# One decoder step on Trainium2: expert pairs in the order gate/up a, gate/up b, down a, down b

## What is computed

```python
logits = xf @ w_router + b_router
top_logit, top_idx = lax.top_k(logits, 4)
gates = softmax(top_logit)
# for each expert e, on the tokens that chose it:
gu = x_e @ w_gate_up[e] + b_gate_up[e]          # (tokens, 1024) @ (1024, 2048)
g, u = split(gu);  g = min(g, 7);  u = clip(u, -7, 7)
act = (u + 1) * g * sigmoid(1.702 * g)
y_e = act @ w_down[e] + b_down[e]               # (tokens, 1024) @ (1024, 1024)
y[tokens of e] += gates * y_e
x = layer_norm(alpha * x + y)
```

## Time and profile before

| | |
|---|---|
| median of 3 runs | 1364.59 us (1364.25 to 1365.44) |
| profiled execution, its time | 1363.42 us |
| its span, first to last instruction | 1361.6 us |
| mean granted TensorE clock | 0.966 of full |
| TensorE busy | 1213.2 us (89%) |
| VectorE, ScalarE busy | 370.0 us, 204.2 us |
| read from HBM | 479.40 MB, 356 GB/s over the span |

### The profile page before, as it was taken

How to read it: one execution, slowest core, us unless ns; L and a number is a source line. 1 busy time by engine, 2 the same in 40 slices (tenths; PEclk the granted TensorE clock), 3 DMA queues, 4 the chain that set the end, 5 groups by cost and what they waited for, 6 DMA issues and landing times.

```text
span 1361.6 us, 16905 instructions
## 1 busy us (share of the span) xinstructions
PE 1213.2 (89%) x6528; PEld 614.3 (45%) x6528; DVE 370.0 (27%) x910; ACT 204.2 (15%) x337; POOL 39.0 (3%) x62
## 2 busy tenths in 40 slices
PE   7998998898968998989899898998989889898986
PEld 6994445675743343433343333343333334333332
DVE  3646532254252122020221202122020212202024
ACT  3442220213130101101010110101101010110001
POOL 2201000010010000000000000000000000000001
PEclk8998998999989999999999999999999999999999
DMA  9984776169919999999999999999999999999993
GB/s 324 247 269 158 215 253 227 63 254 406 417 66 365 418 418 416 417 417 418 418 419 417 418 417 417 418 418 419 417 418 417 417 417 418 419 418 417 417 416 131
DMA packets 103205, 485.10 MB, mean 356 GB/s; under 512 B 8864, under 2 KB 9204, under 8 KB 69792
## 3 DMA queue, kind: packets, MB, share of 16 engines
q1 hardware_dynamic: 99296, 469.47, 87.0%
q0 software_dynamic: 3872, 15.12, 3.4%
HBM read 479.40 MB, written 5.17 MB: 356 GB/s over the span
## 4 chain that ended last, share of the span: by engine, by line
PE 65%; SPq 17%; DVE 7%; DMA 4%; issue 4%; ACT 2%; DVEq 0%; ACTq 0%
PE ps L1820 23%; PE ps L1842 11%; PE ps L1491 11%; SPq L584 9%; SPq L580 8%; PE ps L1522 5%; PE ps L1852 4%; DMA ring<-in_w_gate_up_dram 4%; PE ps L1792 2%; PE ps L1652 1%; DVE arena L1394 1%; ACT arena L922 1%; DVE arena L1379 1%; DVE arena L1179 1%; DVE arena L1383 1%
## 5 line engine op out<-in xcount | busy, mean ns | idle before, releaser
L1820 PE MATMUL ps<-ring,arena 128*64 128x512 f32 x1536 | 339.2, 594 | 9.9 <-DMA ring<-in_w_gate_up_dram 9.9
L1377 DVE TENSOR_SCALAR arena<-ps 128x512 f32<-128x512 f32 x32 | 22.2, 694 | 701.4 <-PE ps L1820 701.4
L1820 PEld LDWEIGHTS ps<-ring,arena 128*64 128x64 f32 x1536 | 110.8, 137 | 223.4 <-issue 190.1
L1842 PE MATMUL ps<-ring,arena 128*64 128x512 f32 x768 | 170.1, 596 | 23.9 <-ACT arena L922 23.9
L1852 PE MATMUL ps<-arena 128*128 128x264 f32 x256 | 92.1, 506 | 35.0 <-DVE arena L1394 33.6
L1842 PEld LDWEIGHTS ps<-ring,arena 128*64 128x64 f32 x768 | 54.2, 137 | 124.3 <-issue 114.4
L916 ACT ACTIVATE arena<-arena 128x512 f32<-128x512 f32 x32 | 20.2, 632 | 576.1 <-DVE arena L1377 576.1
L1491 PE MATMUL ps<-arena,ring 128*128 128x264 f32 (+1 forms) x384 | 87.6, 389 | 4.4 <-DVE arena L1161 3.7
L1852 PEld LDWEIGHTS ps<-arena 128*128 128x128 f32 x256 | 53.4, 241 | 78.6 <-DVE arena L1394 59.9
L1820 PE MATMUL ps<-late,arena 128*64 128x512 f32 x384 | 85.4, 593 | 0.3 <-DMA late<-in_w_gate_up_dram 0.3
L1491 PEld LDWEIGHTS ps<-arena,ring 128*128 128x128 f32 x384 | 73.6, 192 | 18.9 <-DVE arena L1161 3.9
(11 more groups left out here) (282 smaller groups left out, 979.2 us busy)
## 6 DMA issues: line engine op xcount, KB each, us to landing
ring<-in_w_gate_up_dram SPq DMA_DIRECT2D x192, 1024.0 KB, 19.6
ring<-in_w_down_dram SPq DMA_DIRECT2D x96, 1024.0 KB, 23.9
late<-in_w_gate_up_dram SPq DMA_DIRECT2D x48, 1024.0 KB, 19.2
late<-in_w_down_dram SPq DMA_DIRECT2D x24, 1024.0 KB, 22.8
arena<-in_w_gate_up_dram SPq DMA_DIRECT2D x16, 1024.0 KB, 19.2
ring<-in_w_in_dram SPq DMA_DIRECT2D x12, 1024.0 KB, 17.5
ring<-in_cache_mem_k_dram SPq DMA_DIRECT2D x8, 1024.0 KB, 5.1
ring<-in_cache_mem_v_dram SPq DMA_DIRECT2D x8, 1024.0 KB, 12.5
```

Source lines behind the costliest of these rows:

```text
L1377: nc.vector.tensor_scalar(g2, ps[:, 0, :], 7.0, None, ALU.min).then_inc(e_g2, 1)
L1820: ins = mm(ps[64 * j:64 * j + 64, gu, :], x, w[:, D * gu + 512 * j:D * gu + 512 * j + 512], start=(c < 0), stop=(c == 7), skip_group_check ...
L1842: ins = mm(ps[64 * j:64 * j + 64, 4 + half, :], x, w[:, kk, 512 * half:512 * half + 512], start=(m == 0), stop=(m == 7), skip_group_check= ...
```

## The change

The items of a pair are streamed and used in the order gate/up a (8), gate/up b (8), down a (4), down b (4); before it was gate/up a (8), down a (4), gate/up b (8), down b (4). A function `item_of` translates a place in the stream into expert and item. Since both experts' gate/up results are now alive at once, b's go to the banks 6 and 7 (`6 * a + gu`). The 8 scatter matmuls stand one by one behind the items 1 to 7 of gate/up a and item 0 of gate/up b, the gate transposes behind item 1 of b, and a's `turn_act` behind item 5 of b. After `down` a come `turn_act` b, then the gather (or, in the last pair, five halves of `sum_turned`), then `down` b. VectorE adds the scattered outputs before it clamps a's, and ScalarE copies the gathered tokens after the activation of b. Bytes, matmuls and copies are the same in number.

```diff
+        def item_of(m):
+            two, q = 2 * (m // (2 * PER_EXPERT)), m % (2 * PER_EXPERT)
+            return (two + q // 8, q % 8) if q < 16 else (two + (q - 16) // 4, 8 + (q - 16) % 4)
...
             with dve.Fori(0, pairs) as it:
-                clamp(2 * it)
-                swiglu(2 * it)
                 add_scattered(it)
...
+                clamp(2 * it, 0)
+                swiglu(2 * it)
...
-                clamp(2 * it + 1)
+                clamp(2 * it + 1, 6)
...
                         for j in range(2):
-                            ins = mm(ps[64 * j:64 * j + 64, gu, :], x,
+                            ins = mm(ps[64 * j:64 * j + 64, 6 * a + gu, :], x,
...
+                    if a == 0 and c >= 1:
+                        scatter(it, c - 1)
+                    if a == 1 and c == 0:
+                        scatter(it, DC - 1)
+                    if a == 1 and c == 1:
+                        turn_gates(it)
+                    if a == 1 and c == 5:
+                        pe.wait_ge(e_act, 2 * it + 2)
+                        turn_act()
...
-                gate_up(r, 2 * j)
-                pe.wait_ge(s_first, 16)
...
-                scatter()
...
-                turn_act()
+                gate_up(r, 2 * j, it)
+                gate_up(r, 2 * j + 1, it)
                 pe.wait_ge(e_at_out, 2 * it + 2)
                 down(r, 2 * j)
+                pe.wait_ge(e_act, 2 * it + 3)
+                turn_act()
+                pe.wait_ge(e_u2, 2 * it + 3)
                 if last:
-                    sum_turned(0, 0)
-                    sum_turned(0, 1)
                     pe.wait_ge(e_st_out, 3 * it + 4)
-                    sum_turned(1, 1)
-                pe.wait_ge(e_u2, 2 * it + 2)
-                gate_up(r, 2 * j + 1)
-                if last:
-                    pe.wait_ge(e_u2, 2 * it + 3)
-                    sum_turned(2, 0)
-                    sum_turned(2, 1)
+                    for t, half in ((2, 0), (2, 1), (1, 1), (0, 0), (0, 1)):
+                        sum_turned(t, half)
                 else:
                     pe.wait_ge(e_sel, it + 2)
                     gather()
-                pe.wait_ge(e_act, 2 * it + 3)
-                turn_act()
```

More of the change, by code:

```diff
@@ L492, in reader_done @@
                 eng.wait_ge(s_sav, i // 4 + 1 + (2 if what == "mv" else 0))
+        def item_of(m):
+            two, q = 2 * (m // (2 * PER_EXPERT)), m % (2 * PER_EXPERT)
+            return (two + q // 8, q % 8) if q < 16 else (two + (q - 16) // 4, 8 + (q - 16) % 4)
+        ITEM_AT = {item_of(m): m for m in range(ROUND)}
         def expert_slot(m):
@@ L574, in item_load @@
             def item_load(e0, m):
-                e, i = e0 + m // PER_EXPERT, m % PER_EXPERT
+                k, i = item_of(m)
+                e = e0 + k
                 dst, done = expert_slot(m), expert_landed(m)
@@ L586, in item_read @@
             def item_read(k0, m):
-                k, i = k0 + m // PER_EXPERT, m % PER_EXPERT
+                k, i = item_of(m)
+                k += k0
                 if i < 7:
@@ L916, in pair @@
                     nc.scalar.activation(sg_, g2, ACT.Sigmoid, scale=1.702).then_inc(e_sig, 1)
[L917 to L920, removed]
                     act.wait_ge(e_at, 2 * it + (a + 2))
                     nc.scalar.copy(actT, ps[:, 2, :].rearrange("p (q n) -> p q n", q=4)).then_inc(e_at_out, 1)
+                if not last:
+                    act.wait_ge(e_gx, it + 2)
+                    nc.scalar.copy(xTe, ps[:, 6:8, :].rearrange("p b (c n) -> p (b c) n", n=P)).then_inc(e_gx_out, 1)
                 act.wait_ge(e_dn, 2 * it + 2)
@@ L1372, in _, with clamp @@
                 nc.vector.tensor_copy(SelT[0:NX, half, :], ps[0:NX, 3, 0:T]).then_inc(s_rt_out, 1)
-            def clamp(k):
+            def clamp(k, b):
                 dve.wait_ge(e_gu, k + 1)
-                nc.vector.tensor_scalar(g2, ps[:, 0, :], 7.0, None, ALU.min).then_inc(e_g2, 1)
+                nc.vector.tensor_scalar(g2, ps[:, b, :], 7.0, None, ALU.min).then_inc(e_g2, 1)
                 dve.wait_ge(e_act, k + 1)
-                nc.vector.tensor_scalar(u2, ps[:, 1, :], 7.0, -7.0, ALU.min, ALU.max).then_inc(e_u2, 1)
+                nc.vector.tensor_scalar(u2, ps[:, b + 1, :], 7.0, -7.0, ALU.min, ALU.max).then_inc(e_u2, 1)
             def swiglu(k):
@@ L1806, in _, with gate_up @@
             pe.wait_ge(s_nsw, 4)
-            def gate_up(r, k):
+            def gate_up(r, k, it):
                 a = k % 2
@@ L1813, in gate_up @@
                     if c >= 0:
-                        item_arrived(pe, r, PER_EXPERT * k + c)
-                        w, x = expert_slot(PER_EXPERT * k + c), xTe[:, c, SLOTS * a:SLOTS * a + SLOTS]
+                        m = ITEM_AT[k, c]
+                        item_arrived(pe, r, m)
+                        w, x = expert_slot(m), xTe[:, c, SLOTS * a:SLOTS * a + SLOTS]
                     else:
@@ L1824, in gate_up @@
                         ins.then_inc(e_wu, 1)
-                ins.then_inc(e_gu, 1)
+                    if c == 7:
+                        ins.then_inc(e_gu, 1)
+                    if a == 0 and c >= 1:
[7 more added lines that the diff above has]
+                        turn_act()
             def turn_act():
@@ L1834, in down @@
                 for i in range(4):
-                    item_arrived(pe, r, PER_EXPERT * k + 8 + i)
-                    w = expert_slot(PER_EXPERT * k + 8 + i).rearrange("p (k n) -> p k n", k=2)
+                    item_arrived(pe, r, ITEM_AT[k, 8 + i])
+                    w = expert_slot(ITEM_AT[k, 8 + i]).rearrange("p (k n) -> p k n", k=2)
                     for kk in range(2):
@@ L1844, in down, with scatter, turn_gates @@
                     ins.then_inc(e_du if i < 3 else e_dn, 1)
[L1846 to L1855, removed]
+            def scatter(it, c):
+                half = c // 4
+                if c == 0:
+                    pe.wait_ge(s_first, 16)
+                    pe.wait_ge(s_rt_out, 6)
+                    pe.wait_ge(s_alpha, 1)
+                    pe.wait_ge(e_yb, it + 1)
+                    pe.wait_ge(e_st_out, 3 * it + 1)
+                    pe.wait_ge(e_at_out, 2 * it + 1)
+                if c >= 2:
+                    pe.wait_ge(e_y_out, DC * it + c)
+                mm(ps[:, 2 + c % 2, 0:T], yb[:, half, P * (c % 4):P * (c % 4) + P], SelT[:, half, :],
+                   start=True, stop=True).then_inc(e_y, 1)
+            def turn_gates(it):
+                pe.wait_ge(e_y_out, DC * it + (DC + 1))
+                pe.wait_ge(e_selg, it + 1)
+                for t, (t0, n) in enumerate(TCH):
+                    ins = tp(ps[:, 3, t0:t0 + n], SelG[0:n, t].rearrange("p a s -> p (a s)"), ident[0:n, 0:n])
+                ins.then_inc(e_st, 1)
             pe.sem_inc(e_at, 1)
@@ L1871, in pair @@
                 it = 2 * r + j
-                scattered[0] = DC * it
                 pe.wait_ge(e_gx_out, it + 1)
```

## The result

The changed kernel takes 1357.72 us (median of 5 runs, 1357.14 to 1358.12) against 1364.59 us (now also of 5 runs, 1364.06 to 1365.44): a ratio of 0.9949, 95% interval 0.9935 to 0.9964. That is 6.9 us, where 6.5 were forecast. Of the profiled executions, the span is 1355.3 us (before 1361.6) and the mean granted clock 0.982 (before 0.966).

The account below looks back on a forecast made before the run. The weights' stream was taken to bound the loop, with TensorE's chain at the end. 3.8 us from the stream's start plus 2.7 us from the end gave 6.5 us less, 1358.1 us against 1364.59, range 1355.5 to 1362.0.

Parts of the forecast that it names:

- The stream bounds the loop: Expert loop: the weights' stream at 418 GB/s, 60.2 us for a pair's items, sets the time; TensorE needs less.
- TensorE starts to wait for items: Expert loop: TensorE's waits for DMA begin near 650 us instead of 970.
- The stop goes: First pair: the DMA stop at 426 to 432 us disappears, 3.8 us won, bounds 2.9 and 4.4.
- The margin: First pair: item plus scatter take 2.34 us against a transfer's 2.51, leaving 0.17 us per item.
- signs of being wrong: Profile after: no DMA share under 0.9 from 408 to 1330 us; a stop at 408 to 425 would be wrong.
- The last landing: End of the stream: the last item lands near 1333.8 us, before at 1337.6.
- The end: Last pair: TensorE's 15.4 us chain from item 19 ends 5.2 us behind the last landing, not 7.9; 2.7 us won.
- The middle: Middle of the loop: TensorE's work per pair becomes 52.5 us, worth nothing because the stream covers it.
- A: Rival, first or last pair: only one term comes, 1361.2 or 1360.8 us; chance 0.14.
- B: Rival, loop's stream: eight down items in a row run slower, at 5% 1374.5 us, sign turns at 2.0%; chance 0.07.
- C: Rival, TensorE's clock: waits for single items drop it to 1.2 GHz in the last pair, 1373.5 us; chance 0.05.
- D: Rival, both ends of the loop: hand-overs overlap and the stream's start comes smooth, 1355 us; chance 0.05.

Follow-up runs that it names:

- e4: Two kernels, the changed kernel and the kernel before, each with every gather of the loop done twice: 1359.25 us and 1397.28 us.
- e7: The changed kernel itself, run again on one chip beside other versions: 1358.34 us, ratio 0.995 to the kernel before.
- e2: The changed kernel with the eight scatters and the gate transposes as one block between gate/up a and gate/up b: 1358.14 us.
- e6: e1 with 34 dummy matmuls put into TensorE's 2.06 us wait for the activation of a: 1361.87 us, ratio 0.9977 to the kernel before.
- e1: The kernel before, items in the old order, with only the scatters put between the items of gate/up a: 1390.54 us, ratio 1.0175.

## Why the prediction was right

*The stream bounds the loop.* Shown by the two e4 kernels, but for some 2 us of the 48 that stay open. TensorE starts to wait for items at 656 us (forecast: near 650).

*The stop goes.* It does, and by bytes in the first 32 us it gave 3.5 us; the forecast was 3.8 with bounds of 2.9 and 4.4. The margin that the prediction leaned on was mis-sized: a scatter costs 0.64 us between two items, not 0.58, and its neighbour 1.87, not 1.76, so the pace is 2.51 us an item, just what a transfer takes. And one of the prediction's own signs of being wrong came, a share under 0.9 between 408 and 425 us: the dip at 414 to 416 us, (418 - 287) x 2 us = 0.26 MB or 0.6 us. But the pace isn't shown to be its cause. In the second profile of the same kernel (e7) that place is nearly full, and a dip lies earlier:

```profile
412.50:413.50 1.00, 1.00 (x6) 0.49 (x6) 0.24 (x1) 0.00 (x0) 0.00 (x0) 1.00 0.80 209
414.00:416.00 2.00, 2.00 (x10) 0.64 (x8) 0.23 (x1) 0.00 (x0) 0.00 (x0) 1.00 0.98 375
```

e2, whose buffers come free every 1.76 us, moves no more in its first 24 us (331 GB/s) nor in its first 32 (354). What the 3.8 us lack lies elsewhere: in the first 24 us the changed kernel moves 331 GB/s where the kernel before moved 342, which is 0.6 us of stream; 4.1 us of stop less 0.6 are the 3.5. Why these 24 us carry less is open.

*The last landing* was forecast near 1333.8 and came at 1335.0, 2.6 us earlier than before and not 3.8. 3.5 us were won at the start, so 0.9 us went on the way. By bytes it lies in how the stream runs out. Before:

```profile
1335.00:1336.00 1.00, 1.00 (x11) 0.67 (x8) 0.51 (x1) 0.00 (x0) 0.00 (x0) 1.00 0.58 233
1336.00:1337.00 1.00, 0.61 (x5) 0.37 (x4) 0.00 (x0) 0.35 (x1) 0.00 (x0) 1.00 0.27 111
1337.00:1338.00 1.00, 0.71 (x6) 0.71 (x7) 0.00 (x0) 0.23 (x1) 0.00 (x0) 1.00 0.06 16
```

After:

```profile
1331.00:1332.00 1.00, 1.00 (x12) 0.88 (x10) 0.00 (x0) 0.00 (x0) 0.00 (x0) 1.00 0.70 283
1332.00:1333.00 1.00, 1.00 (x7) 0.43 (x8) 0.00 (x0) 0.00 (x0) 0.00 (x0) 1.00 0.56 217
1333.00:1334.00 1.00, 1.00 (x8) 0.33 (x6) 0.00 (x0) 0.00 (x0) 0.00 (x0) 1.00 0.09 25
1334.00:1335.00 1.00, 1.00 (x6) 0.29 (x4) 0.00 (x0) 0.00 (x0) 0.00 (x0) 1.00 0.03 12
```

The share falls below 0.8 some 4 us ahead of the last landing, where it was 2.6 us before. At 418 GB/s the bytes of these stretches would have taken 2.7 us less than they did, and 1.7 us less before: a difference of 1.0 us. The order of the items isn't shown to be the reason. e6 has the old order and a run-out of 3.6 us (its share is 0.68 from 1336 us on, its last landing at 1339.6), so it is rather the one profile of before that is short; against e6 the changed kernel's last landing is 3.5 us earlier, what the bytes of the start say. Why the run-outs differ is open.

*The end.* From item 19 to the end of `down` b I had 15.4 us; it is 1339.1 - 1323.9 = 15.2. But item 19 lands 11.1 us ahead of the last one, not 10.2, because of that slow run-out, and so the end lies 4.1 us behind the last landing, not 5.2. Before it was 7.9, so the term is 3.8 and not 2.7. Taken each by itself, both terms miss their bounds: 2.6 us is less than 2.9, and 3.8 more than 3.4 (and that 3.4 had no ground in the rows it named, since 2.95 us for 24 rows is 0.123 us each, no tighter than the 0.12 of the sum). The two errors are one, in the last landing, and cancel: what the end hangs on is item 19, and that came as forecast, at 1323.9 where 1333.8 - 10.2 = 1323.6 was implied. The sum was right for that reason; the split into its two terms was not. The sum 2.6 + 3.8 = 6.4 us stands beside 6.3 in the spans and 6.5 in the forecast. e6 measures the last pair's part from another side: with the old order and no DMA gain `down` b ends 2.7 us earlier than before, and 4.3 us behind its last landing instead of 7.9.

*The middle.* 53.7 us a pair instead of 52.5, by the dearer scatters. Free, as said.

*The rivals.* A (a term missing): part of its mechanism came, a pace of 2.51 us instead of 2.34 (not its 2.9), and no run shows that it cost anything. B: from 440 to 1330 us the rate is 417 GB/s against 418, no sign of 2%. C: the granted clock is 1.00 from 440 us to the end of the last pair, though TensorE waits for items from 656 us on. That confirms what I set against it, and e1 shows that the mechanism behind C is real, with waits of 0.53 and 2.06 us and not with those of 0.6: it cost 28.7 us there. The Trainium skill, "TensorE: Matmul & The Clock Gate", section "HAM oscillation — how this bites in real kernels", tells of a kernel in which the clock falls anew for every tile, behind a wait for data. e1 agrees in that `down` a is slow in each of the first five pairs (8.5 to 10.0 us), though its waits are for VectorE; the changed kernel's loop, at 1.00 throughout, shows nothing of the kind. D's 1355 us did not come.

## What to carry to other kernels

Where a ring of buffers feeds the matmuls, look for the longest stretch in which no buffer is given back, and compare it with what the stream has in hand there. Here an order that uses all the preloaded items first took the stop away with or without interleaving, and interleaving without it did not. A short wait on TensorE can cost twice, once by itself and again by the clock of what stands behind it; here 2 us of dummy matmuls made a pair 2.5 us shorter (60.4 to 57.9), and on the edge between two bounds (60.4 against 60.2 us) that was 2% of the whole. Read the end from the item on which the last chain hangs, not from the last landing. And before a difference of 1 or 2 us is put down to an edit, see where in the profile it lies: here the loop's start alone wandered by 2.3 us.

## What the runs showed of the hardware

- After waits of 0.53 and 2.06 us with 0.59 us of work between them, the granted clock fell to 0.50 (e1, from within 427 to 428 us until 434), through some 4 us of `down` a's matmuls, and came back by itself. Filling the longer wait kept it at 1.00; waits of 0.5 to 0.7 us between items of 1.9 us of work, from 656 us to the end of the loop, left it there too.
- A float32 matmul 128x264 between two items' matmuls takes 0.64 us and makes the item behind it 0.1 us dearer (1.87 instead of 1.76), against 0.58 in a pair of its own kind.
- The stream of 1 MB loads runs out unevenly: from the fall of the DMA share below 0.8 to the last landing it took 2.6 us in the kernel before, 4 in the changed one and 3.6 in e6.
